# Fetching the token blocks of a mixture-of-experts stage one by one, in the order of need

## The reference

```
gate = jnp.einsum('nd,edf->nef', xf, w_gate)
up = jnp.einsum('nd,edf->nef', xf, w_up)
act = jax.nn.silu(gate) * up * combine[:, :, None].astype(x.dtype)
out = jnp.einsum('nef,efd->nd', act, w_down)
...
return rms_norm(h, norm_final_g)
```

## Time and profile before

| what | value |
|---|---|
| median of three runs | 2459.97 us |
| the profiled execution | 2460.47 us |
| its span, first to last instruction | 2458.7 us |
| PE busy | 2282.9 us (93%) |
| DVE busy | 1238.7 us (50%) |
| ACT busy | 1050.6 us (43%) |
| POOL busy | 641.5 us (26%) |
| mean granted clock of PE | 0.963 |
| first PE work of the experts' stage (line 1314) | 2165.51 us from the start |
| DMA of `xs` | 7 issues, 516 KB each |
| DMA of `mraw` | 168 issues, 512 KB each |

### The profile page before, as it was taken

One profiled execution on the slowest core, in us unless ns is written; L12 is line 12 of the kernel. 1 busy time (PEld: TensorE's weight loads), 2 busy tenths in 40 slices (PEclk: granted clock), 3 DMA queues, 4 the chain that ended last, 5 costly groups with the idle time before them and its releaser, 6 DMA issues.

```text
span 2458.7 us, 31493 instructions
## 1 busy us (share of the span) xinstructions
PE 2282.9 (93%) x12106; PEld 1777.0 (72%) x12106; DVE 1238.7 (50%) x1917; ACT 1050.6 (43%) x1565; POOL 641.5 (26%) x286
## 2 busy tenths in 40 slices
PE   5998999889999999988999989999989999969997
PEld 2776666678888888867656558888877865757776
DVE  3665832253431334236675235525433269259998
ACT  3433831352322333225365144434333268347875
POOL 1220000322232223232300034434454410222133
PEclk8999999889999999988999989999999999979999
DMA  6421032113212231212402323333222321368996
GB/s 249 176 95 43 36 127 78 53 54 127 78 60 64 101 119 61 69 44 99 145 35 84 124 102 95 95 94 103 94 86 92 97 69 46 115 250 318 351 355 257
DMA packets 81181, 291.33 MB, mean 118 GB/s; under 512 B 10729, under 2 KB 13194, under 8 KB 80076
## 3 DMA queue, kind: packets, MB, share of 16 engines
q1 hardware_dynamic: 74192, 257.68, 31.1%
q10 hardware_dynamic: 3964, 17.95, 2.0%
q0 software_dynamic: 2880, 13.68, 1.4%
HBM read 283.50 MB, written 9.48 MB: 119 GB/s over the span
## 4 chain that ended last, share of the span: by engine, by line
PE 81%; DVE 9%; ACT 3%; issue 2%; DMA 2%; POOL 1%; DVEq 1%; SPq 0%; ACTq 0%
PE ps L661 39%; PE ps L708 12%; DVE mlo L2563 4%; PE ps L684 4%; PE ps L1362 3%; PE ps L989 2%; PE ps L769 2%; PE ps L1005 2%; PE ps L942 2%; PE ps L1222 2%; PE ps L1380 2%; PE ps L1078 1%; PE ps L960 1%; DMA wraw<-in_w_all 1%; POOL x L601 1%
## 5 line engine op out<-in xcount | busy, mean ns | idle before, releaser
L595 POOL TENSOR_TENSOR wlo<-wraw,whi 128x1024 fp32r<-128x1024 f32 x208 | 502.4, 2416 | 1343.6 <-ACT whi L1403 703.5
L661 PE MATMUL ps<-hhi,whi 128*128 128x512 f32 x1624 | 592.7, 365 | 3.0 <-DVE hlo L2267 2.0
L661 PE MATMUL ps<-hlo,whi 128*128 128x512 f32 x1624 | 584.6, 360 | 0.0
L661 PE MATMUL ps<-hhi,wlo 128*128 128x512 f32 x1624 | 581.8, 358 | 0.0
L661 PEld LDWEIGHTS ps<-hhi,whi 128*128 128x128 f32 x1624 | 307.0, 189 | 83.0 <-issue 31.2
L661 PEld LDWEIGHTS ps<-hhi,wlo 128*128 128x128 f32 x1624 | 306.1, 188 | 47.9
L661 PEld LDWEIGHTS ps<-hlo,whi 128*128 128x128 f32 x1624 | 307.0, 189 | 45.6 <-issue 1.0
L1992 DVE SCALAR_TENSOR_TENSOR up<-ps,cconv,up 128x511 f32<-128x511 f32 (+1 forms) x132 | 83.2, 658 | 288.6 <-ACT up L1737 286.1
L2563 DVE TENSOR_TENSOR mlo<-mraw,mhi 128x1024 fp32r<-128x1024 f32 x147 | 206.9, 1437 | 6.0 <-ACT mhi L1851 5.5
L1410 ACT ACTIVATE whi<-wraw 128x1024 fp32r<-128x1024 f32 x132 | 138.8, 1052 | 146.5 <-PE ps L708 120.3
L708 PE MATMUL ps<-alo,whi 128*128 128x512 f32 (+1 forms) x528 | 188.1, 356 | 0.0
(11 more groups left out here) (346 smaller groups left out, 3706.2 us busy)
## 6 DMA issues: line engine op xcount, KB each, us to landing
wraw<-in_w_all SPq DMA_DIRECT2D x288, 512.0 KB, 3.5
mraw<-in_w_moe SPq DMA_DIRECT2D x168, 512.0 KB, 5.6
mraw_b<-in_w_mod SPq DMA_DIRECT2D x10, 512.0 KB, 15.3
fl<-in_four ACTq DMA_DIRECT2D x2, 2048.0 KB, 8.3
hd<-in_hyf POOLq DMA_DIRECT2D x2, 2048.0 KB, 9.1
hi<-in_hyi ACTq DMA_DIRECT2D x2, 2048.0 KB, 9.7
slot_rows<-in_slot_rows ACTq DMA_DIRECT2D x1, 3612.0 KB, 21.4
xs<-slot_rows POOLq DMA_DIRECT2D x7, 516.0 KB, 12.8
```

Source lines behind the costliest of these rows:

```text
L595: pool.tensor_tensor(wlo[:, slot, :], wraw[:, AT_W[n] % RING, :], whi[:, slot, :].bitcast(F32), ALU.subtract).then_inc(lo_split, 1)
L661: m = pe.matmul(ps[:, bank + b, 0:w], a, r[:, c0:c0 + w], start=k == 0 and q == 0, stop=k == KT - 1 and q == 2)
```

## The change

The blocks are fetched in the order 1, 0, 2, 3, 4, 5, 6 (`BLOCK_ORDER`), all on `blocks_in`. `block_landed(b)` gives the count at which block b is in. A fetch waits on POOL until the one before it has landed. The first stands where block 0's stood; each of the others stands behind one more `mlo` of POOL. `turn_block` waits for its own block, and `y_add` waits for its block in all seven.

```diff
+    BLOCK_ORDER = [1, 0] + list(range(2, BLOCKS))
+
+    def block_landed(b):
+
+        return sem("blocks_in"), 16 * (BLOCK_ORDER.index(b) + 1)
...
+        def fetch_block(n):
+            b = BLOCK_ORDER[n]
+            if n:
+                pool.wait_ge(sem("blocks_in"), 16 * n)
+            pool.dma_start(xs[:, b, :], slots_d[b * P:b * P + P, :]).then_inc(sem("blocks_in"), 16)
+
         mlo(*list(M_POOL)[0])
         pool.wait_ge(sem("rows_placed"), 16 * (TX // P))
-        pool.dma_start(xs[:, 0, :], slots_d[0:P, :]).then_inc(sem("first_block_in"), 16)
-        for b in range(1, BLOCKS):
-            pool.dma_start(xs[:, b, :], slots_d[b * P:b * P + P, :]).then_inc(sem("blocks_in"), 16)
-        for u, j in list(M_POOL)[1:]:
+        fetch_block(0)
+        for n, (u, j) in enumerate(list(M_POOL)[1:]):
             mlo(u, j)
+            if n + 1 < BLOCKS:
+                fetch_block(n + 1)
...
-            pe.wait_ge(sem("blocks_in"), 16 * (BLOCKS - 1))
+            pe.wait_ge(*block_landed(b))
...
-            if b == 0:
-                dve.wait_ge(sem("first_block_in"), 16)
+            dve.wait_ge(*block_landed(b))
```

## The result

The changed kernel takes **2442.13 us** (median of four runs, 2437.98 to 2445.26), against 2459.91 for the kernel before beside it: ratio 0.9923, 95% interval 0.9911 to 0.9935. The ten runs of both have a median of 2444.15 and run from 2437.98 to 2451.00; the 32 runs of the kernel before that were taken beside them and beside e1b to e8 have 2460.11 (2457.80 to 2468.47). So the gain is about **16 us**, where 14.8 were forecast. That lies inside the range; the first four runs by themselves lie just outside it.

What follows compares the result with a forecast made beforehand. DVE and PE were taken to share the bound, DVE slightly ahead, with a hole where PE waits for block 6. 13.4 + 3.6 - 2.2 = 14.8 us off 2459.97 gave 2445.2 us, range 2442.0 to 2452.0.

Steps and rivals of the forecast that it cites:

- Part 1: Block 1, at the head of POOL's queue, lands after 7.0 us; PE's wait goes from 16.2 to about 1 us.
- Part 2: DVE's 13.4 us idle before `hT` go entirely, and the 2.57 + 1.04 us behind the hole too.
- part 3: One weight slab of POOL that ran beside idle DVE now falls beside busy DVE: minus 2.2 us.
- Part 5: Six fetch issues of 0.53 us move between POOL's slabs; `mlo(2, 1)` may start earlier; no gain counted.
- Part 4: POOL waits for each fetch's landing before the next; POOL's idle time covers it, priced at nothing.
- Part 6: Six blocks, 3.17 MB or 8.0 us of all DMA engines, travel beside working engines; priced at nothing.
- Part 7: At `y_add` DVE waits for block 0 at 2242.79, against a landing near 2199; priced at nothing.
- A: Rival: the six blocks push weight slabs back, ACT waits for them, DVE for ACT; gain 6.8 us, 2453.2 us; chance 0.17.
- C: Rival: the hole was the weights' refill, so the wait only moves to ACT; no change, 2459.2 us; chance 0.06.
- B: Rival: block 1 lands late, at 13.9 us, DVE waits until 2199.5 and the restart stays; 2451.7 us; chance 0.08.
- D: Rival: POOL's waits for blocks hold up its weight slabs; 8.2 us slower, 2468.2 us; chance 0.03.
- one more pair of `mlo` of 4.5 us: Sign expected in the changed profile: one more such pair of slabs near 2194.

Runs made afterwards that it cites:

- e1b: The kernel before, all blocks still fetched at once in order 0 to 6, but PE waits for block 1 alone: stage 262.5 us, median 2449.95 us, ratio 0.9958.
- e8: The changed kernel plus a DRAM-to-DRAM copy of 516 KB behind each fetch but the first, not waited for until the end: stage 261.9 us, ratio 0.9948.
- e11: The kernel of e1b profiled a second time: stage 262.0 us, single timed run 2448.62 us.
- e7: The kernel before with all of POOL's slabs cut by DVE: stage 265.7 us, median 2451.30 us, ratio 0.9964.
- e5: The changed kernel with all of POOL's slabs cut by DVE, fetches kept on POOL: stage 249.0 us, median 2436.13 us, ratio 0.9892.
- e9: The kernel before, unchanged, profiled once more: stage 273.9 us, single timed run 2467.26 us.
- e6: The changed kernel, unchanged, measured and profiled a second time: stage 258.8 us, ratio 0.9941.
- e10: The changed kernel, unchanged, profiled a third time: stage 258.5 us, single timed run 2447.26 us.
- e4b: The changed kernel with every block but block 1 fetched twice in turn, POOL waiting for each landing: stage 268.9 us, median 2455.82 us, ratio 0.9974.
- e2b: The kernel of e1b with block 1 also issued first, the rest at once: stage 263.0 us, median 2450.41 us, ratio 0.9951.
- e3b: The changed kernel with blocks fetched singly but in order 0 to 6: stage 266.6 us, median 2453.02 us, ratio 0.9966.

## Why the prediction was right or wrong

- **What PE waited for: right.** The named row, the landing of block 6, was the cause. With that wait alone taken away the stage became 12.2 us shorter (e1b, e11).
- **Part 1, block 1's landing: right.** 7.0 us assumed, 6.9 us from 2186.68 to PE's start at 2193.58, some 0.7 us of wait against 1.
- **Part 2, 13.4 + 3.6 us of DVE's idle time: right in size.** It went entirely; the pair without POOL's slabs gives 16.7. Its bound was wrong: with a landing of 9.0 us it said that 13.2 us and the restart would still go. e1b is that case but for a few tenths (8.8 us, from an issue 0.6 us later), and the restart stayed. The reason that it gave for the restart, engines handing `aT` round from a standing start, leaves out PE's clock, which was at 0.50 for part of the same work (4.7 us before and 5.9 in e1b, against 3.2).
- **Parts 3 and 5, what POOL's slabs take from DVE: these are the terms that failed.** The sum had minus 2.2 us for the slab that newly meets a busy DVE and nothing for the slab of unit 2, which starts earlier. The first cost 1.6 us (2.83 in place of 1.21). The second, no longer held behind six issues, took 0.8 us less from DVE than before (8.29 us from first to second `eact`, 9.19 and 8.99 before; without POOL's slabs it is 8.10 in e7 and e5 alike, so it isn't the traffic). Part 5 saw that this slab could start earlier, but asked only whether PE or the ring gains by it. Together that is minus 0.8 us, not minus 2.2, and a sum of 16.2, against the 16.4 us that went ahead of the third `eact`. Over the stage DVE's 147 slabs were busy 205.3, 206.3 and 206.1 us in the changed kernel, 206.9 and 206.4 in the kernel before: no price of 2.2 us shows there either. What decides the price of a single slab (1.6 and 2.7 us in two rows above) wasn't tried.
- **The rest of the difference is chance.** The first profiled execution of the changed kernel gained 18.5 us over that of the kernel before. 1.1 of them lie between the 27th and the 28th `eact`, where e9 has the same 1.1 without any change, and 0.8 between the third and the 27th, which e6 and e10 don't repeat.
- **The rule set against part 3** (the Trainium skill, SBUF — State Buffer, Who interferes with whom: a DVE instruction with two SBUF inputs and a GpSimd one that reads SBUF contend, and the one that comes second waits for the whole of the other) was priced at a POOL slab's whole length each time, 2.4 us or more. On average it was 1.6. The trace bears out that the two hold each other up; a whole slab each time it doesn't.
- **Part 4, POOL's waits for landings: right.** Two fetches waited, 5.9 us in all, and no slab was late. The limit is real: e4b crossed it.
- **Part 6, six blocks of traffic at nothing: right, with less room than was said.** Spread out they cost nothing that shows: from the third to the 27th `eact` it took 219.4 us on average, 219.7 before. At once they cost e2b up to 5.1 us, and 3.17 MB more cost e8 4.0. The reckoning compared means over 224 us (360 GB/s); what matters is the first 60 us, where the engines moved some 409 GB/s and their share was 1.00 or more. The Trainium skill's limit of 358 GB/s for a core (DMA: Bandwidth & Descriptors, Specifications) doesn't bind here: 406 to 410 GB/s stood for 50 us.
- **Part 7, `y_add`'s waits: right.** No wait on a block shows there.
- **The range** was left by 1.0 us at its low end, and that was in good part chance. The low end had already put part 3 at nothing, so that term alone doesn't explain it. It lacked the 0.8 us of part 5, and it gave 1 us to the scatter, from three runs of the kernel before (2.0 us apart); ten runs of the changed kernel lie 13 us apart and 32 of the kernel before 10.7. The first four gave 18.9 us, the next six 14.5, and the 16 us of all ten lie inside.
- **The rivals.** The sign named for A and C, ACT waiting for weights by 5 us or more, came (6.5, 5.3 and 4.9 us in three executions), but DVE waited for ACT's slabs no longer than before: the sign was badly chosen. A showed as a cause only when blocks came at once or traffic was added; B in e3b, 266.6 us for the stage; C didn't happen, since the DMA engines moved some 409 GB/s; D only in e4b. The "one more pair of `mlo` of 4.5 us" was a single slab of 2.83 us.

## What to carry to other kernels

A counter shared by several transfers makes the first user wait for the last of them: give the first its own count, and put it at the head of the queue. Then look at what the other transfers push aside: here order without spacing (e2b) was no better than the wait alone, since the weights ran at half speed meanwhile. And before an instruction is moved to GpSimd to relieve VectorE, measure both side by side: here each slab so moved cost VectorE 1.6 us to save 1.2.

## What the runs showed of the hardware

- **A GpSimd subtraction costs VectorE more than doing it itself.** 128x1024 fp32 from two SBUF inputs: 1.18 us on VectorE, 2.4 us and more on GpSimd, and 1.6 us of delay on a busy VectorE for each.
- **Two queues share the DMA engines by halves.** With blocks and weights both under way in e2b, a weight slab of 0.52 MB came every 2.56 us, 205 of 413 GB/s.
- **TensorE came back at the lower clock behind gaps of 3.3 to 16.2 us, and at the full one behind gaps of 0.65 to 1.5 us.** Four transposes took 1.08 or 1.09 us behind gaps of 3.3 and 3.5 us (e11, e1b), 8.1 us (e3b) and 16.2 us (before), and 0.63 us behind 0.65, 1.23 and 1.54 us (the changed kernel). The granted clock was 0.50 in the first 2.2 us behind the gap of 3.5 us and 1.00 from 6.2 us behind it. The work up to the transposes of `eact` took longer behind the gap of 3.5 us (5.9 us) than behind that of 16.2 us (4.7 us).
- **The part ahead of the stage drifts.** The same code took from 2182.5 to 2191.7 us, more than half of what the change gained; the stage measured by itself scattered by 2.3 us at most.
